# Two groups of tiles instead of three in a decoder step with gathered experts; its convolution on four shifted copies

## What is computed

```
p = rmsnorm(x) @ w_in                    # q, k, v, o (512 wide each), 8 gates, a, g (512 each)
h = mlstm(q, k, v, gates, state) * sigmoid(o)      # 4 heads, chunk by chunk; each chunk needs the one before
u = a * sigmoid(g);  c = depthwise_conv31(history + u) + b
c = silu(group_norm(c))
x = x + concat(h, c) @ w_out
q2 = rmsnorm(x) @ w_query                # 8 heads of 2 x 128
s1, s2 = q2 . keys1, q2 . keys2          # 128 keys each; top 16 of each, top 16 of the sums
out = sum over the 8 x 16 picked experts of softmax(score) * gelu(xn . u_tab[e]) * v_tab[e]
y = rmsnorm(x + out)
```

## Time and profile before

| | |
|---|---|
| three runs | 1902.42, 1884.72, 1897.71 us; median 1897.71 |
| span of the profiled execution | 1716.7 us |
| that execution's own time | not recorded apart; the median is 181.0 us above the span |
| busy: PE, VectorE, ScalarE, GpSimd | 1083.7, 1072.5, 340.7, 1049.9 us |
| DMA | 659.76 MB, mean 384 GB/s |
| of it gathers | 570.49 MB |
| weight units | 144 of 512 KB |

### The profile page before, as it was taken

The page is one execution under the profiler, slowest core; times in us unless marked ns, Lnnn a source line. Parts: engine busy times, 40 slices in busy tenths (PEclk is TensorE's granted clock), DMA queues, the critical chain, the costliest instruction groups (busy, mean ns, idle before and its releaser), DMA issues.

```text
span 1716.7 us, 18323 instructions
## 1 busy us (share of the span) xinstructions
PE 1083.7 (63%) x6277; PEld 663.1 (39%) x6277; DVE 1072.5 (62%) x2724; ACT 340.7 (20%) x884; POOL 1049.9 (61%) x1134
## 2 busy tenths in 40 slices
PE   8898739988899999789843347633333333333344
PEld 8887727856675686566620001100000000000001
DVE  4656699665697387744348584848576766665420
ACT  3332314553231255404110000000000000000000
POOL 2024366665446566656567776777777777777771
PEclk9899879988999999899976669955555566556668
DMA  6759999899999999999999999999999999999996
GB/s 227 262 194 409 400 399 374 336 364 410 394 395 380 409 409 409 409 357 409 409 410 409 409 410 403 387 409 409 409 409 409 409 410 410 409 409 409 409 409 268
DMA packets 182979, 659.76 MB, mean 384 GB/s; under 512 B 22208, under 2 KB 22216, under 8 KB 182760
## 3 DMA queue, kind: packets, MB, share of 16 engines
q0 software_dynamic: 156672, 570.49, 84.0%
q1 hardware_dynamic: 25640, 86.01, 13.4%
q10 hardware_dynamic: 576, 2.10, 0.3%
HBM read 652.96 MB, written 5.16 MB: 383 GB/s over the span
## 4 chain that ended last, share of the span: by engine, by line
DMA 33%; POOL 20%; PE 19%; DVE 16%; issue 9%; ACT 2%; POOLq 0%; ACTq 0%; DVEq 0%
DMA ring<-in_u_experts,expert_idx 15%; POOL ring L635 13%; DMA ring<-in_v_experts,expert_idx_by_token 7%; PE pp L676 7%; DVE ring L1131 6%; PE y L951 4%; DMA u_prompt<-in_u_experts,expert_idx 2%; POOL C_sample L635 2%; PE pp L686 2%; PE a L951 2%; POOL w_ring L635 2%; DMA act_T<-in_v_experts,expert_idx_by_token 2%; DMA sig_o_T<-in_u_experts,expert_idx 1%; DMA ring<-in_v_experts,expert_idx 1%; DMA w_ring<-in_u_experts,expert_idx 1%
## 5 line engine op out<-in xcount | busy, mean ns | idle before, releaser
L1131 DVE SCALAR_TENSOR_TENSOR ring<-ring,x_normed 128x1024 f32<-128x1024 f32 x472 | 568.7, 1219 | 364.9 <-DMA ring<-in_u_experts,expert_idx 360.3
L635 POOL DMA_INDIRECT ring<-in_u_experts,expert_idx x472 | 450.4, 954 | 303.6 <-issue 109.0
L951 PE MATMUL y<-ring,z_columns 128*32 128x512 f32 x1080 | 266.6, 793 | 208.5 <-DMA ring<-in_v_experts,expert_idx_by_token 175.5
L635 POOL DMA_INDIRECT ring<-in_v_experts,expert_idx_by_token x308 | 296.4, 962 | 153.7 <-issue 76.9
L676 PE MATMUL pp<-act_T,w_ring 128*128 128x128 f32 (+2 forms) x1728 | 294.9, 330 | 37.5 <-ACT region L1731 8.8
L676 PEld LDWEIGHTS pp<-act_T,w_ring 128*128 128x128 f32 x1728 | 262.9, 198 | 76.3 <-issue 49.5
L951 PE MATMUL y<-C_sample,z_columns 128*32 128x512 f32 x224 | 166.3, 956 | 27.3 <-DMA ring<-in_v_experts,expert_idx_by_token 13.2
L951 PEld LDWEIGHTS y<-ring,z_columns 128*32 128x32 f32 x1080 | 52.6, 130 | 330.4 <-issue 327.4
L951 PE MATMUL a<-ring,z_columns 128*32 128x512 f32 x248 | 147.5, 827 | 35.5 <-DMA ring<-in_v_experts,expert_idx 26.1
L951 PE MATMUL a<-w_ring,z_columns 128*32 128x512 f32 x100 | 76.8, 1026 | 116.7 <-DMA ring<-in_v_experts,expert_idx_by_token 103.5
L686 PE MATMUL pp<-w_ring,act_T 128*128 128x128 f32 (+1 forms) x832 | 104.7, 287 | 27.5 <-DVE scratch L1331 11.3
(11 more groups left out here) (337 smaller groups left out, 1700.8 us busy)
## 6 DMA issues: line engine op xcount, KB each, us to landing
w_ring<-in_w_all SPq DMA_DIRECT2D x136, 512.0 KB, 7.1
ring<-in_u_experts,expert_idx POOLq DMA_INDIRECT x472, 10.8
ring<-in_v_experts,expert_idx_by_token POOLq DMA_INDIRECT x308, 10.5
ring<-in_w_all SPq DMA_DIRECT2D x8, 512.0 KB, 9.9
x_res<-in_x_prompt SPq DMA_DIRECT2D x4, 512.0 KB, 7.3
C_sample<-in_state_C SPq DMA_DIRECT2D x4, 512.0 KB, 13.6
out_C_s<-C_sample ACTq DMA_DIRECT2D x4, 512.0 KB, 11.0
out_y_p<-x_res SPq DMA_DIRECT2D x16, 128.0 KB, 5.4
```

The lines of the kernel that those rows point to most:

```text
L635: pool.indirect_dma_start(out=slot[s], out_offset=None, in_=a["u_experts"] if kind == "u" else a["v_experts"], in_offset=bass.IndirectOffs ...
L951: ins = pe.matmul(total[low:low + 32, half * 512:(half + 1) * 512], zcols[:, part % 2, lo:lo + 32], rhs, start=False, stop=True, skip_grou ...
L1131: dve.scalar_tensor_tensor(out=slot[s], in0=slot[s], scalar=1.0, in1=xn_now[:, :], op0=ALU.mult, op1=ALU.mult, accum_out=dots[:, part % 4, ...
```

## The change

The tiles go in two groups, (1) and (2, 3, 4, 0), so 96 weight units are read. The second pass is 384 + 32 = 416 columns wide; buffers grow and are shared anew: the convolution's inputs, its tap weights and the sample state share `C_sample` one after the other, the sample state is loaded after the last convolution chunk, the two ffn gains and the copy of the sample's normed x lie in `v_rows`, so the gain is loaded twice, and `gain_y` after the sample state is written. Tiles 2, 3, 4, 0 are chunked one after the other (`MIX`), while the experts keep their `ORDER`. u pick 128, tile 2's first, needs scores of the second pass, as before. The extra slots are 13, from u pick 192 on. Tiles 2 and 3 now use the second sum. Of the eight lists three pairs are left (`DVE_STEPS` and `DVE_BY`, `PE_BY`, `ACT_STEPS` and `ACT_BY`): the steps are spelled out (d dot product, r a piece of routing, g gates, f a tile's end), and the counts say how far at each point.

In the second pass the convolution runs on four copies of its input, each shifted by one more row, for 32 channels at a time: a matmul has 4 shifts x 32 channels on its 128 rows and 32 output columns, so 8 matmuls with the input moved on by 4 cover 31 taps for 32 channels, and four of these with different output columns make a chunk. ScalarE makes the copies (16 a chunk), VectorE the taps.

```diff
-GROUPS = [(1,), (2, 0), (3, 4)]
+GROUPS = [(1,), (2, 3, 4, 0)]
-WIDTH = [128, 128 + NS, 256]
+WIDTH = [128, 384 + NS]
+MIX = [1, 2, 3, 4, 0]
-SECOND_SUM = (0, 4)
+SECOND_SUM = (2, 3)
-STATES_AT = FIRST[2] + PART
-WIDER_AT = FIRST[3] + 2 * PART
-JOIN_AT = [("u", STATES_AT)] * 2 + [("u", WIDER_AT)] * 14
+WIDER_AT = FIRST[2] + 2 * PART
+JOIN_AT = [("u", WIDER_AT)] * 13
-LATE_PICKS = [FIRST[GROUPS[1][0]]]
+LATE_PICKS = [FIRST[2]]
...
+DVE_STEPS = ("r8 d10 r5 d26 g1 d14 r5 d5 r1 d4 r1 d1 r1 d2 r1 d4 r1 g1 d30 g1 d32 g1 r5 f1 d4 r1 d6 r4 d26 g1 d14 "
+             "r5 d5 r1 d5 r1 d1 r1 d3 r1 d1 g1 d3 r1 d3 r1 d5 r1 d1 r1 d3 r1 d3 r1 d3 r1 d5 r1 d1 r1 d3 r1 d2 r1 "
...
@@ sync @@
-            load_w(36, N_W)
+            load_w(36, N_W + 12)
+            sp.wait_ge(hist_copied, 1)
+            sp.dma_start(o["conv_s"], hist_out).then_inc(out_s, 16)
+            sp.wait_ge(u_ready, 2 * len(CONV_RUNS))
+            sp.dma_start(o["conv_p"], up[:, :, MAX_P:MAX_P + HIST]).then_inc(out_p, 16)
+            load_w(N_W + 12, N_W + N_IN + 4)
+            filled(sp, ("conv", 1, CC - 1))
+            sp.wait_ge(conv_s_done, 1)
+            sp.wait_ge(hist_copied, 1)
+            sp.wait_ge(scores_read, 4)
+            sp.wait_ge(out_p, 16)
             for h in range(H):
                 sp.dma_start(Cs[h], a["state_C"][:, h, :, :]).then_inc(ld_state, 16)
...
+            sp.wait_ge(att_done, 5)
+            sp.dma_start(gains[1], a["norm_ffn"].broadcast_to([128, D])).then_inc(ld_gain, 16)
...
+            load_w(N_W + N_IN + 4, N_W + N_IN + N_OUT + 4)
             sp.wait_ge(xs_ready, 1)
             for s in range(1, 4):
                 sp.dma_start(xs[NS * s:NS * (s + 1), :], xs[0:NS, :]).then_inc(spread_x, 16)
...
+            load_w(N_W + N_IN + N_OUT + 4, N_W + N_IN + N_OUT + 8)
+            sp.wait_ge(out_c, 16 * H)
+            sp.dma_start(gain_y, a["norm_final"].broadcast_to([128, D])).then_inc(ld_gain_y, 16)
+            load_w(N_W + N_IN + N_OUT + 8, 2 * N_W)
...
@@ tensor @@
+            def conv(c):
+
+                pe.wait_ge(taps_made, c + 1)
+                pe.wait_ge(shifts_made, c + 1)
+                p = job(("conv", 1, c))
+                for g in range(TAP_GROUPS):
+                    for i in range(4):
+                        ins = pe.matmul(p[32 * i:32 * i + 32, 0:MAX_P], taps_4[:, i * TAP_GROUPS + g, :],
+                                        shifted[:, i, SHIFTS * g:SHIFTS * g + MAX_P],
+                                        start=(g == 0), stop=(g == TAP_GROUPS - 1), skip_group_check=True)
+                ins.then_inc(pp_full, 1)
                 keep()
...
             project_in(1, 20, 24)
-            conv(1, 0)
             within_chunk(2)
-            conv(1, 1)
+            conv(0)
             heads_back(2)
-            conv(1, 2)
+            scores_in_chunk(3)
+            conv(1)
+            keys_by_rows(3)
+            from_state(3)
+            within_chunk(3)
+            by_group("mean", "rest", 0)
+            conv(2)
+            heads_back(3)
+            scores_in_chunk(4)
+            conv(3)
...
             query_head(1, head)
-
-            inputs(2)
-            project_in(2, 0, 16)
...
@@ vector: the convolution's taps @@
+                shape = [128, SHIFTS * TAP_GROUPS, 32]
+                dve.tensor_tensor(taps_4, bc(fold[:, :], 1, shape), bc(w_4[:, c, :, :].rearrange("p i g -> p (i g)"), 2, shape),
+                                  ALU.mult).then_inc(taps_made, 1)
...
@@ scalar @@
+            def shifts(c):
...
+                for s in range(SHIFTS):
+                    n = min(MAX_P + TAPS - SHIFTS + 1, MAX_P + HIST - s)
+                    for i in range(4):
+                        ins = A(shifted[32 * s:32 * s + 32, i, 0:n], up[32 * i:32 * i + 32, c, s:s + n], ACT.Copy)
...
+            def conv_out(c):
+                job = ("conv", 1, c)
                 filled(act, job)
+                act.wait_ge(scores_read, c + 1)
+                A(cv[1][:, c, 0:MAX_P], bank(job)[:, 0:MAX_P], ACT.Identity, bias=bdw[:, c:c + 1]).then_inc(free(job), 1)
+                if c + 1 < CC:
+                    shifts(c + 1)
...
+            project_in(1, 18, 24)
+            conv_out(0)
+            exp_rows(3)
+            conv_out(1)
+            exp_scores(3)
+            conv_out(2)
+            exp_rows(4)
+            exp_scores(4)
+            conv_out(3)
             exp_rows(0)
...
+            step.done()
+            stream(len(STEPS))
```

In `DVE_BY` and `PE_BY` all of tile 1's dot products are in by the step after the fourth tile's chunk, its last quad by output unit 6, and no step of tile 2 comes on VectorE before the last step of the pass, on PE and ScalarE before the last query head. ScalarE's squares of all four tiles now stand ahead of the spread of the transposed x:

```diff
+            act.wait_ge(mix_c, 3 * CC)
+            square2(0, region[:, 0:D])
             sums_sqrt(0, 1, NS)
-            for t in (2, 0):
+            act.wait_ge(cs_new, 2 * H)
+            for t in GROUPS[1]:
+                square2(t, region[:, (t + 1) * D:(t + 2) * D]) if t else None
+            sums_sqrt(2, 5, 128)
+            for t in GROUPS[1]:
                 for half in range(2):
                     spread_T("x2T", t, half, gffn)
```

More of the change, by code:

```diff
@@ new lines, in order_of_banks @@
+    inputs(0)
+    project(0, 0, 4)
+    jobs += [("gates", 0), ("gffn",)]
+    project(0, 4, 15)
+    jobs.append(("mean", "first", 0))
+    project(0, 15, 16)
+    jobs.append(("cols", 1))
+    project(0, 16, 18)
+    jobs.append(("kTr", 1))
+    project(0, 18, 20)
+    jobs.append(("var", "first", 0))
+    project(0, 20, 24)
+    jobs += [("dens", 1), ("mean", "first", 1), ("var", "first", 1), ("hT", 1)]
+    outputs(0)
+    inputs(1)
+    jobs.append(("gates", 1))
+    project(1, 0, 16)
+    jobs.append(("cols", 2))
@@ L160, in order_of_banks @@
+    outputs(1)
     return {name: n for n, name in enumerate(jobs)}
@@ L439, in build @@
         w_before, w_times, w_last = [], [], {}
-        for n in range(3 * N_W):
+        for n in range(2 * N_W):
             w_before.append(w_last.get(w_place(n)))
@@ L1510, in experts_of @@
                     step.done()
-                    between()
+                    if h != heads[-1]:
+                        yield
                 p = parts_before(t) + part
@@ L1522, in experts_of, with all_parts @@
                     dve.transpose(idxT[:, now], idx[:, now]).then_inc(picked_v, 1)
-            def between():
-                p = routed[0]
-                stretch[0] += 1
-                while p and done[0] < ROUTE_DOTS[p][stretch[0]]:
-                    dot_product(done[0])
             def routing(t, part):
-                stretch[0] = 0
                 for heads in ((0,), (1,)) if (t, part) == (1, 0) else ((0, 1),):
-                    top_lists(t, part, heads)
-                    candidates(t, part, heads)
-                    experts_of(t, part, heads)
-                routed[0] += 1
+                    yield from top_lists(t, part, heads)
+                    yield from candidates(t, part, heads)
+                    yield from experts_of(t, part, heads)
+                    if heads[-1]:
+                        routed[0] += 1
+                    yield
+            def all_parts():
+                for p in range(N_PART):
+                    t = tile_of(PART * p)
+                    yield from routing(t, p - parts_before(t))
+            routes = all_parts()
             dve.wait_ge(ld_x[1], 16)
@@ L1913, in _ @@
             gate_rows(0)
+            spread_w()
             filled(act, ("gffn",))
```

565 lines of the change are left out of this document (241 added, 324 removed), and 39 rows, old and new, of tables (ACT_BY, DOTS_BY, DVE_BY, DVE_STEPS).

## The result

The changed kernel takes 1938.4 us (median of 4 runs, 1935.6 to 1944.9) where the kernel before takes 1899.7 on the same chip (4 runs, 1884.7 to 1902.4): ratio 1.0236, 95% interval 1.019 to 1.0283. It is slower, by 39 us between the medians and by 45 us if the ratio is taken.

The account below looks back on a forecast made before the run. DMA was taken as the bound, the time set by when tile 2's first gather starts and what DMA carries afterwards. 626 us to that gather, 1121 after it and 181 outside the span gave 1928 us, range 1890 to 1972.

Parts of the forecast that it names:

- four signs of being wrong: GpSimd's idle under 20 us, middle not near 131, later gathers not at 1.27 us, or time outside the span moving.
- slower still: Rival: the middle costs both old middles, 188 us; first gather of tile 2 at 683, time 1985 us; chance 0.15.
- The start: Second pass's gates start at 150 us: the old 145.28 plus two more tiles of inputs at 2.4 us each.
- The middle: Last input unit to first output unit of the second pass: 131 us, with bounds of 93 and 188.
- The outputs: Second pass's eight output units with sample state instructions and 12 quads of experts: 94 us, ending at 562.
- DMA before tile 2: Tile 1's gathers run at 385 GB/s, the last landing at about 533 us; then about 65 us of DMA dry.
- Weights behind tile 2: 28 fewer weight units read after 576 us, at 1.28 us each: 36 us gained.
- The start of tile 2: After tile 2's first gather, routing and a gate wait in VectorE's line hold up slots: 15 us lost.
- The sum's base: 181 us between span and median time taken as fixed, outside the span, and added to 1747.
- DMA stays the bound up to the outputs' end: Rival: middle 110 us or less, outputs end near 546, tile 2 starts at 597 to 610; 1899 to 1912; chance 0.19.
- the faster one: Rival: DMA finishes tile 1 by 512, middle takes its lower bound of 93, first gather at 589; 1876 us; chance 0.15.
- Wide units that cost little: Rival: 416-column units cost hardly more than 256-column ones, 2.1 us off each of 36 units; 1891 us; chance 0.03.

Follow-up runs that it names:

- before, second profile: The kernel before, unchanged, profiled again beside the follow-up experiments: time 1893.85 us, span 1891.8 us.
- after's second profile: The changed kernel, unchanged, profiled again on the same chip as the kernel before: 1929.41 us, span 1927.7 us.
- Run 8: Changed kernel with 2 of the 8 tap groups of its convolution on TensorE and ScalarE's copies cut to 32 columns: 1925.65 us, ratio to before 1.0191.
- run 2: Changed kernel reading only an eighth of each of the second pass's 48 weight units: 1934.8 us, ratio to before 1.0208.
- run 3: Kernel before reading only an eighth of each of the third pass's 48 weight units: 1887.9 us, ratio 0.9973.
- Run 11: Kernel before with 8 of the 31 taps in each of its eight convolution chunks: 1863.4 us, ratio 0.9833.
- run 4: Changed kernel with tile 2's first 12 u gathers issued before its routing, using tile 1's indices: 1935.75 us, ratio to before 1.0243.
- run 9: Changed kernel with tile 2's first gates made inside the seventh query head and ScalarE's squares of tiles 2 to 4 after the spread: 1918.6 us, ratio 1.0132.
- run 10: Kernel of run 9 plus the 12 early gathers of run 4, against the kernel before: 1907.9 us, ratio 1.009.
- run 5: Changed kernel with ScalarE making the gates of tile 2's first part after the seventh query head, not all eight: 1921.9 us, ratio to before 1.0169.

## Why the prediction was right, and where its steps were off

The forecast was 1928 in 1890 to 1972, slower with 0.60; measured 1938.4, 2.0 to 2.4% slower where 1.6% was forecast. The direction and the mechanism held: the second pass became TensorE's and the chain's, GpSimd stood 88.8 us before tile 2 (60 or more forecast), released by the index cast. The number is nearer than its parts deserve, and that is luck: the first gather came 68 us later than forecast, what follows it in the span took 1243 us for 1121 (+122), and the 181 us set outside the span were 1.8 (-179). Of the forecast's own four signs of being wrong, three came: the middle wasn't near 131, the gathers didn't go at 1.27 us, and the time outside the span moved. Its first gather is even later than the 683 of its rival "slower still". Its terms:

| term | forecast, us | after, us |
|---|---|---|
| gates of the second pass start | 150 | 169.9 |
| to the first unit | 9 | 7.4 |
| input units | 178 | 177.0 |
| middle | 131 | 171.1 |
| outputs | 94 | 107.4 |
| turn to the queries | 16 | 15.4 |
| two heads | 31 | 29.2 |
| evacuation and routing | 17 | 16.8 |
| tile 2's first gather | 626 | 694.2 |

- **The start** was worked out soundly but from a rare execution. In before, second profile, the gates stand at 166.98 and not at 145.28, as its one line shows:
```profile
166.98 4.01 PE L715 MATMUL pp<-act_T,w_gates 128*36 128x160 f32 x16 [1.12 <-ACT act_T L1684]
```
 After is 2.9 us later than that (7.5 in its second profile); 4.8 were forecast for the two more tiles.
- **The middle** is the term that was off most: 171 (166 in the second profile) for 131, inside the bounds of 93 and 188. Part of it has the cause of the start: the two old middles are 228 us and not some 190 in before, second profile, and 131 stretched by that fifth would be 158 (my estimate). The rest I read as hops between engines that my walk took too short. The four tiles came back at 383, 443, 486 and 521 us in after's second profile, 60, 44 and 34 us from one to the next where 46, 34 and 29 were forecast. Run 8 says that the convolution is 10 to 15 us of it; that the rest is the chain follows from the walk through the trace and wasn't tested.
- **The outputs** took 107 for 94: TensorE was busy 97 of them, 12 quads of experts and units of 7.4 us with short waits with no releaser between them.
- **DMA before tile 2.** The forecast let tile 1's gathers run at the old 385 GB/s and land at 533, ahead of TensorE. They went at 321 GB/s with a share of 0.86, and the last left at 604.5, while TensorE was in the sixth of the eight output units, where its program has the quads that free their slots. Before, second profile, has 355 GB/s there. The forecast's picture of DMA waiting only behind its last byte was wrong. It can have moved tile 2's date only by some us: in the middle TensorE waited 8.8 us for v's and VectorE 9.6 us for u's, in the outputs TensorE never.
- **Weights behind tile 2** (36 us forecast as gained) failed as a step: runs 2 and 3 put the bytes of 48 units at 0 and 5 to 9 us. The gain in their place is real, 34 to 45 us from tile 2's first gather to the end against 20 forecast, but most of it isn't bytes: the third pass's work on the engines is gone too. Run 11 shows 18 us for the convolution's thinned part; that the rest belongs to its units, steps and heads is what is left over, not shown.
- **The start of tile 2**: 15 us forecast for it, with a gate wait of 12. The wait was 23.8 us (16.1 in the second profile), and runs 4, 9 and 10 together show that it decides what the early gathers are worth:
```profile
789.69 0.17 DVE L1069 RECIPROCAL z_sum<-z_sum 128x2 f32<-128x2 f32 x1 [23.82 <-ACT dots L1905]
```
 But before has it as well (31.3 us at 716 in its second profile), so it is no cost of the change. The prediction counted it as new; in the profile that it read, the same step stands at 643.74 with no wait in front.
- **The sum's base** failed. "Fixed, outside the span" is 1.8 us. It did little harm because from number 469 on both kernels make the same gathers at the same 1.42 us, and before number 469 the slower execution lengthens before too (39 + 64 us).
- So the errors in the difference cancel in part: tile 2 starts 80 us later (50 forecast), what follows is 34 to 45 us shorter (20 forecast).

The rivals: "DMA stays the bound up to the outputs' end" asked for a middle of 110 or less, the faster one for 93. Neither came; DMA was at 0.82 in the middle. "Slower still" (middle 188, 1985) was 17 us of middle away, nearer than the faster ones. Wide units that cost little are refuted: 5.85 us at 416 columns are 1.57 times the 3.72 of 256 and 2.85 times the 2.05 of 128. The Trainium skill ("TensorE: Matmul & The Clock Gate", Back-to-back issue gap) gives 131 ns at 512 columns, without naming the operands' size; the row has 366 ns at 416 (5.85 / 16), for 4-byte operands. The trace disagrees, and the straight line through the earlier trace rows held to 0.01 us.

## What to carry to other kernels

Merging passes saves weight traffic only where DMA sets the pace; look for the wait that frees the next transfer, since here 22 MB were worth 0 to 9 us while a convolution with 63 us less of TensorE's work was worth 46. A profile can be of an execution that is not like the timed ones: when span and time differ by a tenth, as here (1716.7 and 1897.7), profile once more before anything is added up. When a merged pass serializes four chains that ran two and two, walk through the chain tile by tile, and count every hop high. A stall that is filled may be worth nothing until the next wait in line is gone too: try both together before either is called harmless.

## What the runs showed of the hardware

- The same program's gathers (128 rows of 4 KB) went at 1.271 us each in one execution (409 GB/s) and at 1.42 in all the others profiled (370 GB/s), whatever else was loaded. The Trainium skill ("DMA: Bandwidth & Descriptors", Specifications) has some 358 GB/s as HBM's limit for a core, half of what a stack gives its two cores; slices of 409 to 413 are above that, in both kernels. The profile has this core only, so whether a neighbour was reading isn't shown, and what makes the rare execution fast is open.
- In the heads after tile 2's first gathers TensorE stands for 14.05 us (at 765 in after) and 16.21 (run 5), and ScalarE with it, with no releaser shown, while DMA is full (a share of 1.02 or more in both stops). The cause is open.
- 4 x 8 matmuls that each use 32 columns of the array, for 384 columns, take 6.9 us a chunk (27.4 / 4), where 31 full ones take 22.5 (90.1 / 4).
